# Two transformer blocks on one core: the first stage of the first block is put in another order

## The reference

```
x  (256 x 1024)
first block:
  xn = rmsnorm(x, norm_mix);  q, k, v of 2 x 8 heads of 64 = xn @ w_in;  fa = xn @ (8 more columns)
  logf = log_sigmoid(fa + b_forget);  c = cumsum(logf)
  oa = attention(rmsnorm(qa), rmsnorm(ka), va; bias c_q - c_k, causal)
  ob = attention(rope(rmsnorm(qb)), rope(rmsnorm(kb)), vb; dilated mask)
  h  = x + concat(rmsnorm(oa), rmsnorm(ob)) @ w_out
  h  = h + mixture(rmsnorm(h))       # 32 experts of 1024 x 512, 2 for each token
second block, two layers:
  shift, scale, gate = silu(c) @ ada_w + ada_b      # also for a context row c_ctx
  an attention mixer, then a convolution mixer, each followed by
  a mixture of 16 experts of 1024 x 1024
```

## Time and profile before

| | |
|---|---|
| median of 3 runs | 1875.23 us (1873.79, 1875.23, 1877.55) |
| profiled execution | 1874.42 us, span 1872.6 us |
| PE busy | 1419.9 us, 76% of the span |
| DVE / ACT / POOL busy | 494.0 / 241.9 / 83.0 us |
| HBM read | 714.60 MB, 382 GB/s over the span |
| chain that ended last | DMA 53%, PE 35%, DVE 6%, POOL 2%, issue 2%, ACT 2% |

### The profile page before, as it was taken

One profiled execution on the slowest core, in us unless ns is written; L12 is line 12 of the kernel. 1 busy time (PEld: TensorE's weight loads), 2 busy tenths in 40 slices (PEclk: granted clock), 3 DMA queues, 4 the chain that ended last, 5 costly groups with the idle time before them and its releaser, 6 DMA issues.

```text
span 1872.6 us, 30560 instructions
## 1 busy us (share of the span) xinstructions
PE 1419.9 (76%) x13602; PEld 804.7 (43%) x13602; DVE 494.0 (26%) x1002; ACT 241.9 (13%) x552; POOL 83.0 (4%) x92
## 2 busy tenths in 40 slices
PE   9899986777587899999666557558999756566655
PEld 5455542333243364656333223226867423333322
DVE  4764421111112148943000000003643100000001
...
DMA  9644999999999998589999999999997999999997
GB/s 364 216 177 189 368 398 428 425 427 427 426 421 422 424 353 308 198 358 390 425 428 427 427 426 428 427 427 398 383 396 297 427 427 427 427 427 428 427 427 308
DMA packets 86230, 717.68 MB, mean 383 GB/s; under 512 B 5968, under 2 KB 10832, under 8 KB 49232
## 3 DMA queue, kind: packets, MB, share of 16 engines
...
HBM read 714.60 MB, written 1.05 MB: 382 GB/s over the span
## 4 chain that ended last, share of the span: by engine, by line
DMA 53%; PE 35%; DVE 6%; POOL 2%; issue 2%; ACT 2%; ACTq 0%; SPq 0%; DVEq 0%
DMA ring<-in_moe_w_down 27%; DMA ring<-in_moe_w_gate 11%; DMA ring<-in_w_down 8%; PE bank L1695 5%; PE bank L2545 4%; DMA ring<-in_w_gate 4%; PE bank L506 4%; PE bank L1644 3%; PE bank L1653 3%; PE bank L970 2%; PE bank L1001 1%; PE bank L650 1%; DMA room<-in_rows 1%; PE bank L2305 1%; PE bank L340 1%
## 5 line engine op out<-in xcount | busy, mean ns | idle before, releaser
L1653 PE MATMUL bank<-ring,arena 128*32 128x256 f32 x3840 | 285.6, 451 | 174.7 <-DMA ring<-in_moe_w_up 113.7
L1695 PE MATMUL bank<-ring,arena 128*32 128x256 f32 x2976 | 240.7, 479 | 146.9 <-DMA ring<-in_moe_w_down 119.2
L1653 PEld LDWEIGHTS bank<-ring,arena 128*32 128x32 f32 x3840 | 141.3, 125 | 308.5 <-issue 126.8
L1695 PEld LDWEIGHTS bank<-ring,arena 128*32 128x32 f32 x2976 | 116.3, 132 | 259.4 <-issue 154.8
L1644 PE MATMUL bank<-ring,arena 128*32 128x512 f32 x976 | 134.3, 673 | 72.6 <-DMA ring<-in_w_up 30.4
L1768 DVE TENSOR_TENSOR arena<-arena,bank 128x128 f32<-128x128 f32 (+1 forms) x64 | 22.7, 355 | 499.8 <-PE bank L1653 492.7
L506 PE MATMUL bank<-ring,low 128*128 128x512 f32 (+1 forms) x352 | 150.0, 576 | 2.4 <-DMA ring<-in_w_in 2.4
L1723 PE MATMUL bank<-arena 32*128 32x256 f32 x1024 | 93.8, 437 | 14.6 <-PE bank L1723 10.6
L1779 ACT ACTIVATE arena<-bank 128x256 f32<-128x256 f32 x64 | 24.5, 383 | 557.1 <-PE bank L1709 554.7
L1644 PEld LDWEIGHTS bank<-ring,arena 128*32 128x32 f32 x976 | 28.8, 117 | 153.2 <-issue 99.1
L506 PEld LDWEIGHTS bank<-ring,low 128*128 128x128 f32 x352 | 64.8, 190 | 68.9 <-issue 65.5
...
## 6 DMA issues: line engine op xcount, KB each, us to landing
...
ring<-in_moe_w_down SPq DMA_DIRECT2D x62, 2048.0 KB, 26.7
ring<-in_moe_w_gate SPq DMA_DIRECT2D x58, 2048.0 KB, 26.7
...
ring<-in_ada_w SPq DMA_DIRECT2D x24, 2048.0 KB, 13.4
...
```

The costliest lines, as they stand in the source:

```text
L1653: last = nc.tensor.matmul(GU[up][32 * j:32 * j + 32, 0:QW], xgT[:, x + kk, a:a + C], w[:, kq, j * QW:(j + 1) * QW], start=(kk == 0), stop= ...
L1695: last = nc.tensor.matmul(z_bank(M)[32 * j:32 * j + 32, 0:QW], act_s[:, kk, :], w[:, kq, j * QW:(j + 1) * QW], start=(kk == 0), stop=(kk = ...
```

## The change

- Item 0 is brought as two transfers of 1 MB, channel groups 0 to 3 and 4 to 7, with a semaphore each. PE does groups 0 to 3 of unit 0 and of unit 1, then groups 4 to 7 of unit 0 and of unit 1; each piece waits only for the half of `hT` and of the weights that it reads.
- The forget gate's eight products are written for 32 columns of weights each (the 8 wanted are the last), into the four strips of 32 rows of a bank, two products to a strip, and stand behind unit 1. ACT copies the bank, and one product of 128x8 by 128x256 behind unit 2 adds the strips. DVE's and ACT's steps of the gate move behind the gains of units 2 and 3, from before the first sum.
- The nine gain columns move to the head of PE's program. 9 constant products stand before them and 4 after them, where 26 stood. They multiply by a cell of 1.0 that POOL writes, no longer by a cell of the identity. The load of the last of them counts on `first_loaded` now.
- `ada_add` steps: one between a unit's sum and its gain, so that up to unit 5 it is 12 where it was 14; units 6 and 7 have one more each. By the end of unit 7 it is 20 as before.
- Units 6 to 11 are in three parts, of 3, 3 and 2 products, with one attention step behind each. Of the bias products of unit 11, two stand before the third part.

```diff
-FILL = (20, 5, 5, 25, 26, 22, 12, 7, 4, 9)
+FILL = (20, 5, 5, 25, 9, 22, 12, 7, 4, 9, 4)
...
+        one_cell = columns[0:1, 10 + KD:11 + KD]
...
-            def proj_pe(u, halves=(0, 1)):
+            def proj_pe(u, first, end):
                 pe, un = nc.tensor, units[u]
-                if 0 in halves:
+                if first == 0:
                     if u == 0:
                         for s, v in first_ready:
                             pe.wait_ge(s, v)
                     for s, v in un.get("ready", []):
                         pe.wait_ge(s, v)
+                    if "second_half" not in un:
+                        wait_item(pe, un["item"])
+                    free(pe, u)
+                if first == KD // 2 and "second_half" in un:
+                    for s, v in un["second_half"]:
+                        pe.wait_ge(s, v)
                     wait_item(pe, un["item"])
-                    free(pe, u)
                 a, n = un["cols"]
-                for half in halves:
-                    for k in range(4 * half, 4 * half + 4):
-                        last = nc.tensor.matmul(banks[u % NB][:, 0:n], un["lhs"][:, k, :], ring[un["item"] % SLOTS][:, k, a:a + n],
-                                                start=(k == 0), stop=(k == KD - 1))
-                if 1 in halves:
+                for k in range(first, end):
+                    last = nc.tensor.matmul(banks[u % NB][:, 0:n], un["lhs"][:, k, :], ring[un["item"] % SLOTS][:, k, a:a + n],
+                                            start=(k == 0), stop=(k == KD - 1))
+                if end == KD:
                     last.then_inc(pj, 1)
...
-        units1[1]["ready"] = hT_ready(0)
-        h1 = heads("h1", units1, sq1, qn1, tmp1, hT_ready(0, 0), bank[0:2])
+        for t in range(T):
+            units1[t]["ready"], units1[t]["second_half"] = [(hT_act, t + 1)], [(hT_dve, t + 1)]
+        h1 = heads("h1", units1, sq1, qn1, tmp1, [(half_loaded, 16)], bank[0:2])
...
-        FG_MM, FG_Z, FG_LN, FG_C = range(1, 5)
+        FG_MM, FG_COPIED, FG_SUM, FG_Z, FG_EXP, FG_LN, FG_C = range(1, 8)
         FG = bank[5][0:8, 0:S]
-
-        def forget_pe():
+        fs = h[:, 1, S:2 * S]
+        f_cols = slice(G1 + E1 + 2 * E2 + 8 - C, G1 + E1 + 2 * E2 + 8)
+
+        def forget_strips_pe():
             nc.tensor.wait_ge(const_loaded, 48)
-            for s_, v in hT_ready(0):
-                nc.tensor.wait_ge(s_, v)
             for k in range(KD):
-                last = nc.tensor.matmul(FG, router_sb[:, k, 68:76], hT[:, k, :], start=(k == 0), stop=(k == KD - 1))
+                j = k % 4
+                last = nc.tensor.matmul(bank[5][32 * j:32 * j + 32, 0:S], router_sb[:, k, f_cols], hT[:, k, :], start=(k < 4), stop=(k >= 4))
             last.then_inc(forget_steps, 1)
 
+        def forget_copy_act():
+            nc.scalar.wait_ge(forget_steps, FG_MM)
+            nc.scalar.activation(fs, bank[5][:, 0:S], ACT.Copy).then_inc(forget_steps, 1)
+
+        def forget_sum_pe():
+            nc.tensor.wait_ge(forget_steps, FG_COPIED)
+            nc.tensor.matmul(FG, const("stack")[:, C - 8:C], fs, start=True, stop=True).then_inc(forget_steps, 1)
...
-            nc.tensor.wait_ge(on_steps, 32)
+            nc.tensor.wait_ge(on_steps, 16)
             for k in range(KD + 1):
-                last = nc.tensor.matmul(bank[3][:, k:k + 1], on_row[:, k * P:(k + 1) * P], ident[0:1, 0:1], start=True, stop=True)
+                if k == KD:
+                    nc.tensor.wait_ge(first_loaded, 48)
+                last = nc.tensor.matmul(bank[3][:, k:k + 1], on_row[:, k * P:(k + 1) * P], one_cell, start=True, stop=True)
             last.then_inc(on_steps, 1)
...
+        ADDS_EARLY = (1, 2, 2, 2, 3, 2)
+
         def steps1():
             yield "strips", 0
+            yield "proj", (0, 0, 4)
+            yield "proj", (1, 0, 4)
             for u in range(6):
-                yield "proj", (u, (0, 1))
+                yield "proj", (u, 4 if u < 2 else 0, KD)
                 yield "sum", u
                 if u:
+                    yield "ada_add", 1
                     yield "rope", u - 1
                 yield "gain", u
-                if u == 1:
-                    yield "forget", 0
-                yield "ada_add", 1 if u < 4 else 5
+                if 1 <= u < 4:
+                    yield "forget", u - 1
+                yield "ada_add", ADDS_EARLY[u] - (1 if u else 0)
                 if u >= 2:
                     yield "tr", u - 2
             for u in range(6, 12):
                 s = 3 * (u - 6)
-                yield "proj", (u, (0,))
+                yield "proj", (u, 0, 3)
                 if u > 6:
                     yield "gain", u - 1
                 if u < 8:
@@ -1141,12 +1163,11 @@
                 yield from attend1(s)
                 if u < 8:
                     yield "ada_use", u - 6
-                yield "ada_add", 1
+                yield "ada_add", 2 if u < 8 else 1
                 if u == 11:
                     yield "bias", 0
                     yield "bias", 1
-                yield "proj", (u, (1,))
-                yield "sum", u
+                yield "proj", (u, 3, 6)
                 yield from attend1(s + 1)
                 yield "ada_add", 1 if u < 10 else 2
                 if u > 6:
@@ -1154,6 +1175,8 @@
                 if u == 11:
                     yield "bias", 2
                     yield "bias", 3
+                yield "proj", (u, 6, KD)
+                yield "sum", u
                 yield from attend1(s + 2)
                 yield "ada_add", 1
             for s in range(18, LAST1 + 4):
@@ -1168,16 +1191,18 @@
             pe = nc.tensor
             pe.wait_ge(setup_done, 1)
             keep_pe(FILL[4])
-            pe.wait_ge(first_loaded, 32)
+            gain_cols_pe()
+            keep_pe(FILL[10])
             tr_pe(0, 0, xn_ready(0, 0), AB)
             tr_pe(0, 1, xn_ready(0, 1), own=True)
             for what, i in steps1():
                 if what == "proj":
-                    u, halves = i
-                    if u == 1:
-                        forget_pe()
-                        gain_cols_pe()
-                    h1["proj_pe"](u, halves)
+                    h1["proj_pe"](*i)
+                elif what == "forget":
+                    if i == 0:
+                        forget_strips_pe()
+                    elif i == 1:
+                        forget_sum_pe()
...
-            act.dma_start(on_row[:, D:D + P].rearrange("o (p k) -> o p k", k=KD), cols_in[0:P // KD, a:a + KD].unsqueeze(0)).then_inc(on_steps, 16)
+            act.dma_start(on_row[:, D:D + P].rearrange("o (p k) -> o p k", k=KD), cols_in[0:P // KD, a:a + KD].unsqueeze(0)).then_inc(first_loaded, 16)
             norm_act(0, xn, 0, [(rows_moved[0], 16)])
-            act.wait_ge(first_loaded, 32)
+            act.wait_ge(first_loaded, 48)
...
-            forget_act()
             for what, i in steps1():
                 if what == "sum":
                     h1["sum_act"](i)
+                elif what == "forget":
+                    if i == 0:
+                        forget_copy_act()
+                    elif i == 2:
+                        forget_act()
...
-            forget_dve()
...
                 elif what == "forget":
-                    forget_sum_dve()
-                    gain_cols_dve()
+                    if i == 0:
+                        gain_cols_dve()
+                    elif i == 1:
+                        forget_dve()
+                    else:
+                        forget_sum_dve()
...
-            load(0, 1)
+            for half, landed in enumerate((half_loaded, arrived[0])):
+                of = slice(4 * half, 4 * half + 4)
+                first = w_in[0][:, items[0][1]:items[0][1] + NC].rearrange("(p k) n -> p k n", p=P)
+                sp.dma_start(ring[0][:, of, :], first[:, of, :]).then_inc(landed, 16)
...
+            nc.gpsimd.memset(one_cell, 1.0)```

PE's program from its start to unit 3, before. `columns` are constants, `h` the normalized rows, `low` is `hT`, `router_sb` holds the gate's columns:

```order
L340 MATMUL bank<-columns 128x128 x26
L352 MATMUL bank<-room,h 128x128 x16
L506 MATMUL bank<-ring,low 128x512 x8
L738 MATMUL bank<-low,router_sb 8x256 x8
L908 MATMUL bank<-room,arena 128x1 x9
L506 MATMUL bank<-ring,low 128x512 x16
L618 MATMUL bank<-room,arena 128x128 x4
```

27 lines of the change are left out of this document (14 added, 13 removed).

## The result

| | before | after |
|---|---|---|
| median of the runs | 1875.43 us (5 runs, 1873.79 to 1877.99) | 1861.24 us (5 runs, 1859.72 to 1866.30) |
| profiled execution | 1874.42 us, span 1872.6 | 1860.74 us, span 1858.9 |
| ratio after / before | | 0.9928, 95% interval 0.9915 to 0.9942 |

The changed kernel is faster: by 14.2 us between the medians, by 0.72% (13.5 us) by the ratio. The forecast was 1861.0 (1856.5 to 1867.5). The two profiled executions differ by 13.68 us, the forecast's sum was 13.35.

The account below looks back on a forecast made before the run. The weight stream bounds nearly everywhere, released by the first stage's path, mostly PE's. Gains 2.1 + 4.25 + 3.5 + 3.9 less 0.4 make 13.35 us off 1874.42: forecast 1861 us, range 1856.5 to 1867.5 (8 in 10).

Parts of the forecast that it names:

- What bounds: Whole kernel: weight stream sets the end; each microsecond off the first stage's path lets the stream come one microsecond earlier.
- rival (c): PE's saving is hidden and the stream sets the end as before: 1874 to 1875 us; chance 0.06.
- Start: Start of unit 0's projections: with item 0 in halves PE starts at 10.7 instead of 12.81, 2.1 us gained.
- the page's rule: Head: clock follows how busy the array recently was, so slow pace is likely; sum 1.2 us smaller.
- start and clock together: Head: 2.1 us gained by the earlier start, less 0.4 us lost to a slow clock.
- A first record of L511 after 12.5: Sign at unit 0's start that the forecast is wrong; 10.7 would show it right.
- Gate and columns: Between units 0 and 1: columns leave the path, gate strips run beside each other; 4.25 of 5.65 us gained.
- rival (b): Halves land together, or strips run one after another: 1866 us with both, 1863.5 with one; chance 0.11.
- Unit 3 to 7: Mainly unit 6: the wait before `ada_sum 0` and waits of scores for a maximum shrink, 3.5 of 3.91 us gained.
- rival (a): DVE takes PE's place as the bound of units 3 to 7: 1865.5 us; chance 0.13.
- Units 7 to 11: Products between attention steps remove most PE waits in units 7, 8, 9 and 11: 3.9 us gained.
- Later clock: Stretch after unit 11, at granted clock 0.58 before: 3.2 us could be won or lost; taken as 0.

Follow-up runs that it names:

- old_adds: The kernel after with the additions of `ada_w` distributed as before, five at once in units 4 and 5, none before the rope; 1864.87 us, ratio 0.9942.
- before_again: The kernel before, without an edit, traced a second time; 1877.24 us (one run).
- laid_out: The kernel after with gain columns brought ready in the constants' array, none made by PE, and 20 constant products at the head; 1861.44 us, ratio 0.9908.
- gate_eight: The kernel after with the gate's eight products 8 columns wide in one strip, without ACT's copy and the adding product; 1862.89 us, ratio 0.9918.
- after_again: The kernel after, without an edit, run and traced again; 1863.72 us (6 runs), ratio 0.9927.

## Why the prediction was right, and where not

**What bounds.** Right: a microsecond gained in the first stage is one gained in the stream. The lead of 16.0 us stands unchanged through 467 us of weights; 13.9 of it reach the end, since 2.1 are lost later. The issue that answers to the earlier trace rows came 16.0 earlier (forecast 13), and rival (c), the saving hidden by the stream, is out.

**Start, 2.1 forecast, 0.70 measured, and in part of the executions negative.** This is the step that failed. Two things in it. First the length of PE's own work at the head: I let columns and constants end at 8.18. The nine constants took 3.95 where I had 3.4, then PE stood 0.64 for the row, the columns took 2.16 as in the earlier trace rows, to 7.7 where I had 7, and the four constants ended at 9.5. Second the clock. Stretches of the kernel after at the head:

```profile
6.00:7.00 1.00, 1.00 (x11) 1.00 (x11) 0.47 (x1) 0.26 (x1) 0.62 (x2) 1.00 1.08 323
...
8.00:9.00 1.00, 1.00 (x7) 1.00 (x6) 0.57 (x1) 0.00 (x0) 0.40 (x1) 0.50 1.03 399
```

In this execution the granted clock is 1.00 while the columns run and 0.50 from about 8 to 11.3 us, behind the one-column products, and the transposes take 2.92 us where they took 1.95. In the late course the low pace of the program's start isn't left at all until unit 0. The forecast had given this half a chance, at 1.2 us. It came in both courses: 1.7 us in the early one, 0.97 in the transposes (2.92 - 1.95) and 0.70 in the four constants (1.86, and 1.16 in `old_adds`, where the clock fell behind them), and unit 0 another 1.6 later in the late one (13.71 - 12.11). I had argued that 2.4 us without work ahead of unit 0 slowed nothing before; `before_again`, with 2.50 us of it and unit 0 at 8.80, shows that this was one execution. The Trainium skill, page "TensorE: Matmul & The Clock Gate", section "The HAM clock gate", says that how many products run slow at the start differs from run to run of one kernel; the trace agrees, with 2.16 and 4.00 us for the same eighteen records. By the page's rule, 1.2 us less than mine, start and clock together would be 0.5, and it was the better one for this term.

In the early course it hardly reached the time, for a reason the forecast also missed: the first addition's weights land at 27.8 to 28.2 (forecast 26.6), and so a start before about 12.1 was worth nothing. In the late course 1.6 us do reach `ada_sum 0` (62.19 against 60.58). A first record of L511 after 12.5 was a sign of being wrong; four of the six traces with this head show it.

**Gate and columns, 4.25 forecast, 3.97 measured on PE.** Right in size: strips beside each other (1.07, forecast 0.95), so rival (b)'s second half is out (its first half too: in `laid_out` unit 0 starts at 11.45, and item 0 as a whole landed at 12.68 before); the adding product took 0.53 (34.60 - 34.07, forecast 0.45). But `gate_eight` shows that about half of the strips' part was PE's slack.

**Unit 3 to 7, 3.5 forecast, 3.07 measured.** DVE and PE meet, as rival (a) had it in its mildest form: 0.83 of waiting, a little above the 0 to 0.6 given. DVE's timeline shows how the addition went into the wait for POOL:

```profile
36.56 0.68 DVE L543 TENSOR_REDUCE small<-arena 128x8 f32<-128x512 f32 x1
37.27 0.17 DVE L269 TENSOR_SCALAR small<-small 128x8 f32<-128x8 f32 x1
37.35 1.28 DVE L411 SCALAR_TENSOR_TENSOR room<-ring,condT,room 128x1024 f32<-128x1024 f32 x1
38.55 0.69 DVE L605 TENSOR_TENSOR arena<-arena 128x512 f32<-128x512 f32 x1
40.15 0.69 DVE L563 TENSOR_TENSOR arena<-bank,small 128x512 f32<-128x512 f32 x1 [0.92 <-POOL small L279]
```

The wait of 1.52 in the earlier trace rows is 0.92 with 1.28 + 0.69 us of work in front of it, where it was 0.69. The addition took 1.28 here, not 1.75, but it was not free: POOL's root took longer beside it. POOL's timeline before and after:

```profile
43.54 2.01 POOL L278 TENSOR_TENSOR small<-small,columns 128x8 f32<-128x8 f32 x1 [3.56 <-DVE small L268]
```

```profile
37.52 2.60 POOL L279 TENSOR_TENSOR small<-small,columns 128x8 f32<-128x8 f32 x1 [0.30 <-DVE small L269]
```

In `old_adds`, the kernel after without this addition, the root takes 2.01 again. So DVE's way from sum to scaling is 3.59 us in place of 3.01, and an addition in the wait costs 0.6 us of it. The forecast had only the other direction, POOL slowing DVE.

**Units 7 to 11, 3.9 forecast, 5.02 measured; and the thirds as a whole 9 us.** I left a part of each wait standing, out of caution, though DVE's and ACT's busy time in the earlier trace rows left room. Every wait but 0.16 in unit 7 went. Undoing the thirds costs 5 to 6 us of waits over all six units, so they carried a part of what the sum had under unit 6. Of the 9 us in the times, the rest is clock and noise as far as is known.

**Later clock, 0 forecast (between -3.2 and 3.2), +3.2 up to 190 us.** It stands at the edge of the bounds, and most of it is luck: behind `ada_sum 0` the kernel after lost nothing to the clock, and `after_again` and five more with thirds lost 3.4 us, as much as before. I had called the sign open, and it is.

Second block: -2.1, not foreseen, and open.

The total came out within 0.3 us because misses cancelled. Against the forecast's terms the first pair of traces has, in us gained, -1.0 for the start, -0.3 and -0.4 for the next two, +1.1 for the units 7 to 11, +3.2 for the clock and -2.1 in the second block. The terms of order and waits sum to 12.8 of the 13.35; that the total agrees to 0.3 us is luck. The chance of 0.91 for faster by over 0.2% was borne out by terms that did not depend on the head.
